# Middle up projection as seven half-size products per pair, from its seventh pair on

## The chip, the cores and the metric

One Trainium2 chip, one of its cores. The metric is device time of one execution in microseconds (us), lower is better. The kernel before has a median of 2146.22 us over 3 runs (2146.05 to 2146.76).

## The reference, cut to what matters

The reference is two transformer blocks in float32 on 512 tokens of width 1024. It has three feed-forward layers; the change is in the second of them, the first of block two:

```python
D_FF_2 = 2816

def swiglu(x, w_gate, w_up, w_down):
    return (jax.nn.silu(x @ w_gate) * (x @ w_up)) @ w_down

def second_block(x, ffn1_norm, ffn1_w_gate, ffn1_w_up, ffn1_w_down, mix_norm, w_in, ...):
    h = rms_norm(x, ffn1_norm[l])
    x = x + 0.5 * swiglu(h, ffn1_w_gate[l], ffn1_w_up[l], ffn1_w_down[l])   # up1, down1
    h = rms_norm(x, mix_norm[l])
    z = h @ w_in[l] + b_in[l]                                               # wq, wk, wv, ...
    ...
    h = rms_norm(x, ffn2_norm[l])
    x = x + 0.5 * swiglu(h, ffn2_w_gate[l], ffn2_w_up[l], ffn2_w_down[l])   # up2, down2
    return rms_norm(x, final_norm)
```

## The kernel before, in words

**Number format.** Every dense product is three matmuls: weights and activations are each split into a rounded part and a rest ("hi" and "lo", type fp32r), and hi·hi, hi·lo and lo·hi are summed in PSUM (`dense`, L965, with the matmuls at L1034, L1037 and L1038; L1007, L1010 and L1017 for the four chunks that run abreast). TensorE gets the products in program order.

**Weights.** They come as a stream of 512 KB slabs (8 tiles of 128x128). SyncE loads slab after slab into four raw buffers (L803) and waits until the one four slabs ago was split (`wait_raw_free`, L686). ScalarE rounds a slab into `w_hi` (L1759, `feed_to`) and GpSimd subtracts to get `w_lo` (L880). Five slabs of `w_hi`/`w_lo` form a ring. ScalarE's instruction order is written out by hand: `silu_of(c)` (L1944) first feeds slabs up to chunk 2c+3, then waits for its input.

**The up projection of a feed-forward.** 44 output chunks of 128 rows, in 22 pairs (gate, value). A chunk is 8 tiles times 3 matmuls on 512 columns. Chunks 0 to 3 run abreast (k outermost), the others one by one, each with one slab. The input is written before its norm factor is known, so VectorE multiplies each output by that factor (`gate_of` L2674, `value_of` L2679), ScalarE takes the silu (L1952), VectorE the product (L2686), ScalarE rounds it into `a_hi` (L1942) and VectorE makes `a_lo` (`low_a`, L2670). Six PSUM banks are used in turn (L717).

**The seven-product form.** The last feed-forward, `up2`, does its pairs from the fifth on in another way (`paired`, L1045): the 256-token halves of the input and the k-halves of the two weight columns form a 2x2 block product, which is done in seven products of half the size in place of eight (each 4 tiles times 3 matmuls on 256 columns, L1058 to L1060). It needs sums and differences of the weight halves, made for each pair (VectorE `pair_one`, `pair_two`, `pair_four`, L2635 to L2652, and the rests at L2657; GpSimd `pair_pool`, L818, the difference "three" at L836 and four rests at L822; ScalarE seven roundings at L1765), and sums of the input halves, made once: VectorE `input_sums` (L2620, L2630), ScalarE `sum_hi_of` (L1794, L1797), GpSimd four rests `s_lo` (L831), which stand in GpSimd's order ahead of the first pair's "three". It also needs the input with its norm factor in it: `scale_input` (L2609, L2612) writes `u_all`, ScalarE rewrites `u_hi`, VectorE rewrites `u_lo` (`input_lo`, L2614, L2618). Outputs from the sixth pair on are kept whole and split late (`apart`, L1990 and L2718), so the down projection reads hi and lo the other way round there (`turned_from`, L966).

Both helpers have a branch for a layer whose input is rewritten only ahead of its first seven-product pair (`unscaled == paired_from`, L1964, L1979, L2708, L2711, L2713); the kernel before does not take it. In it, ScalarE does for the last pair ahead of the switch, in this order (L1969 to L1986):

```python
if c == paired_from - 1:
    pair_raw(p, 2); pair_three(p); pair_two(p); pair_one(p); pair_four(p)
silu_of(c)
if c == paired_from - 1:
    pair_raw(p, 6); pair_raw(p + 1, 0)
    ...
    f(u_hi[:, i, :], u_all[:, i, :], ACT.Copy)      # for the 8 parts
```

`pair_three` waits for GpSimd's "three"; VectorE's `gate_of` of that pair stands behind its `pair_four_lo` (L2705, L2707). TensorE's first seven-product pair waits for its banks, one of which holds that pair's gate chunk (L1068), and for the first four parts of the rewritten `u_lo` (L1073).

Of the kernel before, what the change touches and what calls it, by code (L numbers as in the profile page):

```python
# [27 lines left out]
DC = D // P  # L28
# [16 lines left out]
FC = FF // P  # L45
# [5 lines left out]
KEPT_FROM = 5  # L51
# [59 lines left out]
NSLABS = -(-TILES // SLAB)  # L111


PAIRED = {"up2": (4, FC)}
PAIRS = [(name, c) for name, (lo, hi) in PAIRED.items() for c in range(lo, hi)]
LAYER_OF = {"up": 0, "up1": 1, "up2": 2}
BLOCKS = 7
# [85 lines left out]
def build(nc, t):  # L203

    ctx = ExitStack()
    with ctx:  # L206
# [13 lines left out]
        u_hi = at("u_hi", 72 * KB, [DC, S], F32R)  # L220
        u_lo = at("u_lo", 88 * KB, [DC, S], F32R)
# [106 lines left out]
        r_sb = arena("r_sb", 86, [S])  # L328
# [557 lines left out]
        def _(pe):  # L886
# [829 lines left out]
            stay_busy(10)  # L1716
            sum_last("post2")
            stay_busy(15)
            dense("up1", u_hi, u_lo, (u_ready, 4 * DC), row="pre2", row_at=(4, 4))
            dense("down1", a_hi, a_lo, (a_ready, FC))  # L1720
            dense("wq", u_hi, u_lo, (u_ready, 5 * DC), row="pre3", row_at=(0, 2), again=6 * DC)
            dense("wk", u_hi, u_lo)
            dense_tokens("wv", 2)
            window()
# [13 lines left out]
                    pe.wait_ge(mh_ready, 8)  # L1738
                dense(f"proj_m{m}", m_hi, m_lo)
            dense("out", mg_hi, mg_lo, (mg_ready, 0))  # L1740
            dense("up2", u_hi, u_lo, (u_ready, 7 * DC), row="pre4", row_at=(0, 2), again=8 * DC, upto=8)
            paired("up2", 8 * DC)
            dense("down2", a_hi, a_lo, (a_ready, 2 * FC), row="pre5", row_at=(DC - 1, FC - 2), turned_from=KEPT_FROM)
            stay_busy(7)
            sum_last("pre5")
# [3 lines left out]
        def _(act):  # L1749
# [102 lines left out]
            def rewrite_hi(k0, name, read, scaled, sums=False):  # L1852

                slabs = (START[name][0] + 4 * DC - 1) // SLAB + 1
                for c in range(DC):
                    feed_to(slabs + 1 + c // 2)
                    act.wait_ge(ux_done, k0 + c + 1)
                    if c < DC - 2:
                        act.wait_ge(u_read, read + c + 1)
                    else:  # L1860
                        act.wait_ge(dense_done, group_of(name, 0 if c == DC - 2 else 3))
                    f(u_hi[:, c, :], scaled[c % len(scaled)], ACT.Copy).then_inc(u_part, 1)
                for i in range(4 if sums else 0):
                    sum_hi_of(name, i)
# [490 lines left out]
            factor("post2", misc[2], misc[2])  # L2355

            late_act(2, 16, "ffn1", "up1")
            ffn_swiglu(1, "up1")
            late_act(3, 24, "mix2", "wq", "down1")
            rewrite_hi(DC + 4, "wq", DC - 2, [slot[4][:, :], slot[5][:, :]])  # L2360
            act.dma_start(wvb[:, :], t["wvb"]).then_inc(c_loaded, 16)
            act.dma_start(band[:, :], t["band"]).then_inc(c_loaded, 16)
            for c in range(8):
# [167 lines left out]
                    act.wait_ge(mg_in, m)  # L2531
                    f(mg_hi[:, m - 1, :], ma[:, m - 1, :], ACT.Copy).then_inc(mg_part, 1)
            late_act(4, 32, "ffn2", "up2", "out")
            rewrite_hi(2 * DC + 4, "up2", 2 * (DC - 2), [u_all[:, c, :] for c in range(DC)], sums=True)
            ffn_swiglu(2, "up2", *PAIRED["up2"], 2)
            norm_act(5, 40, "down2")

# [2 lines left out]
        def _(dve):  # L2540
# [7 lines left out]
            def rewrite(gain, k0, factor, scaled):  # L2548

                for c in range(DC + 1):  # L2550
                    if c < DC:
                        if c >= 2:
                            dve.wait_ge(u_ready, k0 + c - 1)
                        STT(scaled[c % 2][:, :], h[:, c, :], V(gain, c), factor[:, :], ALU.mult, ALU.mult)\
                            .then_inc(ux_done, 1)
                    if c >= 1:
                        dve.wait_ge(u_part, k0 + c)
                        TT(u_lo[:, c - 1, :], scaled[(c - 1) % 2][:, :], u_hi[:, c - 1, :].bitcast(F32),
                           ALU.subtract).then_inc(u_ready, 1)
# [54 lines left out]
            def input_lo(k0):  # L2614

                for c in range(DC):
                    dve.wait_ge(u_part, k0 + c + 1)
                    TT(u_lo[:, c, :], u_all[:, c, :], u_hi[:, c, :].bitcast(F32), ALU.subtract).then_inc(u_ready, 1)  # L2618
# [161 lines left out]
            def add_half(name, scale, norm, late=None):  # L2780

                for c in range(DC):
                    if c >= 2:
                        add_squares(norm, c - 1)
                    dve.wait_ge(dense_done, group_of(name, c))
                    STT(h[:, c, :], out_bank(name, c)[:, :], scale, h[:, c, :], ALU.mult, ALU.add).then_inc(h_ready, 1)  # L2786
                    if late:
                        late_lo(c, *late)
                if norm not in LAST_APART:
                    add_squares(norm, DC - 1)  # L2790
# [414 lines left out]
            TT(sq[(DC - 1) % 3][:, :], mo_a[:, DC - 1, :], mo_a[:, DC - 1, :], ALU.mult).then_inc(ms_sq, 1)  # L3205
            post_apply(2, "ple_post", mo_a, "pre2", "ffn1", 4 * DC)
            inverse("pre2")
            ffn_gate(1, "up1")
            add_half("down1", 0.5, "pre3", ("mix2", 5 * DC))
            inverse("pre3")  # L3210
            rewrite("mix2", 6 * DC, r_sb, slot[4:6])
            for c in range(8):
                dve.wait_ge(dense_done, group_of("wq", c))
                if c < 4:
# [177 lines left out]
            for m in range(DC):  # L3392
# [6 lines left out]
                TT(ma[:, m, :], ma[:, m, :], slot[2 + m % 2][:, :], ALU.add).then_inc(mg_in, 1)  # L3399
                dve.wait_ge(mg_part, m + 1)  # L3400
                TT(mg_lo[:, m, :], ma[:, m, :], mg_hi[:, m, :].bitcast(F32), ALU.subtract).then_inc(mg_ready, 1)
            add_half("out", 0.5, "pre4", ("ffn2", 7 * DC))
            inverse("pre4")
            scale_input("ffn2", misc[3])
            input_lo(8 * DC)
            input_sums("up2", 3 * DC + 4)
            ffn_gate(2, "up2", *PAIRED["up2"], 2)
            add_half("down2", 0.5, "pre5")

# [159 lines left out]
```

## Time and profile before

| | us |
|---|---|
| median of 3 runs | 2146.22 |
| span of the profiled execution | 2144.6 |
| time outside that span, by the median | 1.6 |
| `up1`: first matmul of chunk 0 to first of `down1` (two chains of 22 pairs) | 914.7 to about 1155 |
| `up2`: seven-product pairs | 1828.1 to 2011.8 |

Of the profiled execution itself only the span is shown; the 1.6 us are the distance of the median to it. In a timeline row the first number is the start, the second the duration (of a merged row, from the first start to the last end), then engine, line, operation, and in brackets the engine's idle time before it with what ended it.

### The profile page before, as it was taken

The page shows a single profiled execution, that of the slowest core. Times are in us where ns is not written, and L with a number is a line of the kernel's source. Part 1 is how long each engine was busy: PE and PEld are TensorE (multiplying, and loading weights), DVE is VectorE, ACT ScalarE, POOL GpSimd, SP SyncE. Part 2 cuts the span into 40 slices and gives each one's busy share as a digit, 9 for nine tenths or more (in the row PEclk, how much of TensorE's full clock was granted, in tenths as well). Part 3 has the DMA queues.
Part 4 walks back from the last instruction along what each step waited for, and adds up shares of the span by engine and source line. Part 5 has one row for each costly group of instructions (what it writes and reads, how often), then busy time and mean ns, then how long its engine had stood idle before and what let it go on. Part 6 is the DMA issues. An engine that isn't in the chain of part 4 may idle for free. (4 is left out here: it accounts for less than half of the span.)

```text
span 2144.6 us, 29184 instructions
## 1 busy us (share of the span) xinstructions
PE 2122.6 (99%) x11584; PEld 1775.6 (83%) x11584; DVE 1002.8 (47%) x1821; ACT 942.4 (44%) x1630; POOL 946.4 (44%) x441
## 2 busy tenths in 40 slices
PE   9999999999999999999999999999999999999998
PEld 8788877787888888888888888778888888999986
DVE  7684555446655500563332124653744126776611
ACT  7835545545544422442223232662447235545521
POOL 4423322345544443654444344034524445766631
PEclk9999999999999999999999999999999999999999
DMA  4313321232333332222333323023332332333321
GB/s 179 98 50 112 110 69 50 98 113 85 104 94 97 115 102 88 89 89 94 95 97 99 98 89 112 21 79 100 108 89 62 107 93 85 99 103 113 117 92 49
DMA packets 56439, 200.68 MB, mean 94 GB/s; under 512 B 6640, under 2 KB 7536, under 8 KB 55920
## 3 DMA queue, kind: packets, MB, share of 16 engines
q1 hardware_dynamic: 52416, 188.77, 27.8%
q10 hardware_dynamic: 3888, 10.05, 1.4%
q8 instruction: 92, 1.51, 0.3%
q14 instruction: 43, 0.35, 0.1%
HBM read 194.60 MB, written 2.10 MB: 92 GB/s over the span
## 5 line engine op out<-in xcount | busy, mean ns | idle before, releaser
L880 POOL TENSOR_TENSOR w_lo<-raw,w_hi 128x1024 fp32r<-128x1024 f32 x313 | 768.1, 2466 | 1016.0 <-ACT w_hi L1759 988.1
L1759 ACT ACTIVATE w_hi<-raw 128x1024 fp32r<-128x1024 f32 x316 | 326.7, 1051 | 138.2 <-PE dense L1038 84.7
L1034 PE MATMUL dense<-u_hi,w_hi 128*128 128x512 f32 x608 | 237.3, 390 | 0.0
L1038 PE MATMUL dense<-u_hi,w_lo 128*128 128x512 f32 x608 | 236.6, 389 | 0.0
L1037 PE MATMUL dense<-u_lo,w_hi 128*128 128x512 f32 x584 | 227.2, 389 | 0.0
L1034 PE MATMUL dense<-a_hi,w_hi 128*128 128x512 f32 x400 | 156.0, 390 | 0.0
L1037 PE MATMUL dense<-a_lo,w_hi 128*128 128x512 f32 x400 | 155.6, 389 | 0.0
L1038 PE MATMUL dense<-a_hi,w_lo 128*128 128x512 f32 x400 | 155.6, 389 | 0.0
L1034 PE MATMUL misc<-u_hi,w_hi 128*128 128x512 f32 x368 | 143.5, 390 | 0.0
L1038 PE MATMUL misc<-u_hi,w_lo 128*128 128x512 f32 x368 | 143.2, 389 | 0.0
L1037 PE MATMUL misc<-u_lo,w_hi 128*128 128x512 f32 x360 | 140.1, 389 | 0.0
L1034 PEld LDWEIGHTS dense<-u_hi,w_hi 128*128 128x128 f32 x608 | 114.1, 188 | 24.3 <-ACT mo_a L2349 0.4
L1038 PEld LDWEIGHTS dense<-u_hi,w_lo 128*128 128x128 f32 x608 | 114.1, 188 | 23.9
L1037 PEld LDWEIGHTS dense<-u_lo,w_hi 128*128 128x128 f32 x584 | 109.6, 188 | 22.8
L2786 DVE SCALAR_TENSOR_TENSOR h<-dense,h 128x512 f32<-128x512 f32 x24 | 16.6, 691 | 212.9 <-PE dense L1038 212.9
L822 POOL TENSOR_TENSOR w_lo<-raw,w_hi 128x512 fp32r<-128x512 f32 x54 | 70.2, 1314 | 56.2 <-ACT w_hi L1765 56.2
L1037 PEld LDWEIGHTS dense<-a_lo,w_hi 128*128 128x128 f32 x400 | 75.1, 188 | 15.9 <-issue 0.2
L1038 PEld LDWEIGHTS dense<-a_hi,w_lo 128*128 128x128 f32 x400 | 75.1, 188 | 15.7
L1034 PEld LDWEIGHTS dense<-a_hi,w_hi 128*128 128x128 f32 x400 | 75.1, 188 | 15.6 <-issue 0.2
L958 PE MATMUL misc<-u_hi,w_hi 128*128 128x512 f32 x192 | 81.6, 425 | 0.0
L1034 PEld LDWEIGHTS misc<-u_hi,w_hi 128*128 128x128 f32 x368 | 69.1, 188 | 14.7 <-issue 0.4
L1038 PEld LDWEIGHTS misc<-u_hi,w_lo 128*128 128x128 f32 x368 | 69.1, 188 | 14.5
(571 smaller groups left out, 5004.7 us busy)
## 6 DMA issues: line engine op xcount, KB each, us to landing
raw<-in_weights SPq DMA_DIRECT2D x352, 512.0 KB, 3.5
h<-in_x SPq DMA_DIRECT2D x4, 512.0 KB, 6.7
alibi<-in_alibi ACTq DMA_DIRECT2D x1, 2048.0 KB, 8.4
h<-in_x ACTq DMA_DIRECT2D x2, 1024.0 KB, 7.1
out<-result SPq DMA_DIRECT2D x8, 256.0 KB, 2.2
p_raw<-in_p ACTq DMA_DIRECT2D x2, 512.0 KB, 3.2
hn<-mqk ACTq DMA_DIRECT2D x4, 256.0 KB, 4.0
mqk<-mqk ACTq DMA_DIRECT2D x4, 256.0 KB, 3.8
```

The costliest lines, as they stand in the source:

```text
L822: nc.gpsimd.tensor_tensor(piece(w_lo, p, i), src, piece(w_hi, p, i).bitcast(F32), ALU.subtract).then_inc(st_pool, 1)
L880: nc.gpsimd.tensor_tensor(w_lo[:, ring(s), :, :], raw[:, s % RAWS, :, :], w_hi[:, ring(s), :, :].bitcast(F32), ALU.subtract).then_inc(w_sp ...
L958: mm(out, hi, src_hi[:, i, :], start=(i == 0), stop=False)
L1034: first = mm(out, hi, x_hi, start=(i == 0), stop=False)
L1037: mm(out, hi, x_lo, start=False, stop=False)
L1038: last = mm(out, lo, x_hi, start=False, stop=(i == k - 1))
L1759: f(w_hi[:, ring(s), :, :], raw[:, s % RAWS, :, :], ACT.Copy).then_inc(w_part, 1)
L2786: STT(h[:, c, :], out_bank(name, c)[:, :], scale, h[:, c, :], ALU.mult, ALU.add).then_inc(h_ready, 1)
```

## The change

`up1` gets the seven-product form from its pair 6 (the seventh) on, so 16 of its 22 pairs; its first 12 chunks stay as they are, on the unscaled input. The branch with `unscaled == paired_from` comes into use, chunk 11 reports its reads of `u_hi` (`last_reads`), `down1` reads kept chunks turned, and the counts of the later semaphores are moved by one rewrite of the input. Since `PAIRED` lists `up1` now, `down1`'s banks become 2, 3, 0, 1 (L726), where they were 3, 0, 1, 2.

```diff
-PAIRED = {"up2": (4, FC)}
+PAIRED = {"up1": (6, FC), "up2": (4, FC)}
...
-            dense("up1", u_hi, u_lo, (u_ready, 4 * DC), row="pre2", row_at=(4, 4))
-            dense("down1", a_hi, a_lo, (a_ready, FC))
-            dense("wq", u_hi, u_lo, (u_ready, 5 * DC), row="pre3", row_at=(0, 2), again=6 * DC)
+            dense("up1", u_hi, u_lo, (u_ready, 4 * DC), row="pre2", row_at=(4, 4), upto=2 * PAIRED["up1"][0],
+                  last_reads=2 * PAIRED["up1"][0] - 1)
+            paired("up1", 5 * DC)
+            dense("down1", a_hi, a_lo, (a_ready, FC), turned_from=KEPT_FROM)
+            dense("wq", u_hi, u_lo, (u_ready, 6 * DC), row="pre3", row_at=(0, 2), again=7 * DC)
...
-            ffn_swiglu(1, "up1")
+            ffn_swiglu(1, "up1", *PAIRED["up1"], PAIRED["up1"][0])
...
-            ffn_gate(1, "up1")
-            add_half("down1", 0.5, "pre3", ("mix2", 5 * DC))
+            ffn_gate(1, "up1", *PAIRED["up1"], PAIRED["up1"][0])
+            add_half("down1", 0.5, "pre3", ("mix2", 6 * DC))
```

The lines left out move semaphore counts of later stages (`rewrite_hi`, `rewrite`, `input_lo`, `input_sums`, the `dense` and `paired` calls of `up2`) and nothing else.

## Rows read from the trace of the kernel before

**Rows 1.** The page: busy time, share of the span and instructions of each engine.
```profile
PE 2122.6 (99%) x11584; PEld 1775.6 (83%) x11584; DVE 1002.8 (47%) x1821; ACT 942.4 (44%) x1630; POOL 946.4 (44%) x441
```

**Rows 2.** Busy time by stretch: `up1` with whole products, `up2` with seven (columns PE, PEld, DVE, ACT, POOL, clock, DMA).
```profile
942.00:982.00 40.00, 40.00 (x179) 33.09 (x178) 14.85 (x21) 15.21 (x21) 19.40 (x9) 1.00 0.36 111
1850.00:2000.00 150.00, 150.00 (x1252) 150.00 (x1251) 104.36 (x194) 73.58 (x149) 100.05 (x74) 1.00 0.33 103
```

**Rows 3.** VectorE's timeline: the same step of consecutive pairs, `up1` and `up2`.
```profile
965.41 0.70 DVE L2677 TENSOR_TENSOR dense<-dense,r_sb 128x512 f32<-128x512 f32 x1 [2.70 <-PE dense L1038]
976.29 0.70 DVE L2677 TENSOR_TENSOR misc<-misc,r_sb 128x512 f32<-128x512 f32 x1 [2.70 <-PE misc L1038]
...
1860.19 0.42 DVE L2727 TENSOR_TENSOR slot<-misc,slot 128x256 f32<-128x256 f32 x1 [0.81 <-PE misc L1060]
1870.27 0.42 DVE L2727 TENSOR_TENSOR slot<-dense,slot 128x256 f32<-128x256 f32 x1 [0.81 <-PE dense L1060]
```

**Rows 4.** VectorE's timeline in `up1`: after the second pair's product, and the fourth pair's gate.
```profile
947.78 0.68 DVE L2672 TENSOR_TENSOR a_lo<-slot,a_hi 128x512 fp32r<-128x512 f32 x1
950.43 0.69 DVE L2672 TENSOR_TENSOR a_lo<-slot,a_hi 128x512 fp32r<-128x512 f32 x1
```

**Rows 5.** VectorE's timeline ahead of `up2`'s pairs: scaled input, rewritten rests, sums, first difference.
```profile
1790.65 5.36 DVE L2612 SCALAR_TENSOR_TENSOR u_all<-h,vec,misc 128x512 f32<-128x512 f32 x8 [2.69 <-ACT misc L1933]
1795.93 3.40 DVE L2618 TENSOR_TENSOR u_lo<-u_all,u_hi 128x512 fp32r<-128x512 f32 x4
...
1808.35 1.21 DVE L2630 TENSOR_TENSOR s_all<-u_all 128x1024 f32<-128x1024 f32 x1
...
1813.00 0.69 DVE L2677 TENSOR_TENSOR dense<-dense,r_sb 128x512 f32<-128x512 f32 x1
...
1820.55 2.90 DVE L2641 TENSOR_TENSOR misc<-raw 128x512 f32<-128x512 f32 x1
...
1824.68 1.72 DVE L2672 TENSOR_TENSOR a_lo<-slot,a_hi 128x512 fp32r<-128x512 f32 x1
```

**Rows 6.** ScalarE's timeline ahead of `up2`'s pairs: sums rounded, weight parts, silu.
```profile
1810.85 3.33 ACT L1797 ACTIVATE s_hi<-s_all 128x1024 fp32r<-128x1024 f32 x3 [0.20 <-DVE s_all L2630]
...
1824.62 0.63 ACT L1765 ACTIVATE w_hi<-slot 128x512 fp32r<-128x512 f32 x1 [2.27 <-POOL slot L836]
...
1827.83 0.60 ACT L1765 ACTIVATE w_hi<-misc 128x512 fp32r<-128x512 f32 x1 [1.60 <-DVE misc L2652]
```

**Rows 7.** ScalarE's timeline in `up1`: slabs of chunks 10 and 11 rounded.
```profile
956.27 2.00 ACT L1759 ACTIVATE w_hi<-raw 128x1024 fp32r<-128x1024 f32 x2
```

**Rows 8.** GpSimd's timeline: adds beside VectorE, chunk 9's slab, then `up2`'s sums and "three".
```profile
917.31 10.24 POOL L860 TENSOR_TENSOR h<-h,slot 128x512 f32<-128x512 f32 x6 [11.81 <-DVE slot L2591]
...
951.25 2.39 POOL L880 TENSOR_TENSOR w_lo<-raw,w_hi 128x1024 fp32r<-128x1024 f32 x1 [4.59 <-ACT w_hi L1759]
...
1812.08 10.80 POOL L831 TENSOR_TENSOR s_lo<-s_all,s_hi 128x1024 fp32r<-128x1024 f32 x4 [4.81 <-ACT s_hi L1797]
1822.85 1.74 POOL L836 TENSOR_TENSOR slot<-raw 128x512 f32<-128x512 f32 x1
```

**Rows 9.** TensorE's timeline in `up1`: the first matmuls of chunks 9 and 12.
```profile
965.21 0.39 PE L1034 MATMUL dense<-u_hi,w_hi 128*128 128x512 f32 x1
...
981.53 0.39 PE L1034 MATMUL dense<-u_hi,w_hi 128*128 128x512 f32 x1
```

**Rows 10.** The end: busy time by stretch after the last matmul, columns as in rows 2.
```profile
2135.20:2140.30 5.10, 0.00 (x0) 0.00 (x0) 3.78 (x6) 1.24 (x2) 0.00 (x0) 1.00 0.43 161
2140.30:2144.60 4.30, 0.00 (x0) 0.00 (x0) 1.58 (x3) 0.00 (x0) 0.00 (x0) 0.50 0.80 297
```

**Rows 11.** TensorE's timeline in `up2`: the longest of four idle times among its pairs.
```profile
1848.40 0.35 PE L1058 MATMUL dense<-s_hi,w_hi 128*128 128x256 f32 x1 [0.37 <-DVE slot L2767]
```

**Rows 12.** Timeline of all engines where `down1` ends and `wq` begins.
```profile
1275.49 0.69 DVE L2786 SCALAR_TENSOR_TENSOR h<-dense,h 128x512 f32<-128x512 f32 x1 [12.12 <-PE dense L1038]
...
1275.74 0.39 PE L1007 MATMUL dense<-u_hi,w_hi 128*128 128x512 f32 x1
```

More of the change, by code:

```diff
@@ L1740, in _ @@
             dense("out", mg_hi, mg_lo, (mg_ready, 0))
-            dense("up2", u_hi, u_lo, (u_ready, 7 * DC), row="pre4", row_at=(0, 2), again=8 * DC, upto=8)
-            paired("up2", 8 * DC)
+            dense("up2", u_hi, u_lo, (u_ready, 8 * DC), row="pre4", row_at=(0, 2), again=9 * DC, upto=8)
+            paired("up2", 9 * DC)
             dense("down2", a_hi, a_lo, (a_ready, 2 * FC), row="pre5", row_at=(DC - 1, FC - 2), turned_from=KEPT_FROM)
@@ L2357, in _ @@
             late_act(2, 16, "ffn1", "up1")
-            ffn_swiglu(1, "up1")
+            ffn_swiglu(1, "up1", *PAIRED["up1"], PAIRED["up1"][0])
             late_act(3, 24, "mix2", "wq", "down1")
-            rewrite_hi(DC + 4, "wq", DC - 2, [slot[4][:, :], slot[5][:, :]])
+            rewrite_hi(2 * DC + 4, "wq", 2 * DC - 3, [slot[4][:, :], slot[5][:, :]])
             act.dma_start(wvb[:, :], t["wvb"]).then_inc(c_loaded, 16)
@@ L2533, in _ @@
             late_act(4, 32, "ffn2", "up2", "out")
-            rewrite_hi(2 * DC + 4, "up2", 2 * (DC - 2), [u_all[:, c, :] for c in range(DC)], sums=True)
+            rewrite_hi(3 * DC + 4, "up2", 3 * DC - 5, [u_all[:, c, :] for c in range(DC)], sums=True)
             ffn_swiglu(2, "up2", *PAIRED["up2"], 2)
@@ L3207, in _ @@
             inverse("pre2")
-            ffn_gate(1, "up1")
-            add_half("down1", 0.5, "pre3", ("mix2", 5 * DC))
+            ffn_gate(1, "up1", *PAIRED["up1"], PAIRED["up1"][0])
+            add_half("down1", 0.5, "pre3", ("mix2", 6 * DC))
             inverse("pre3")
-            rewrite("mix2", 6 * DC, r_sb, slot[4:6])
+            rewrite("mix2", 7 * DC, r_sb, slot[4:6])
             for c in range(8):
@@ L3401, in _ @@
                 TT(mg_lo[:, m, :], ma[:, m, :], mg_hi[:, m, :].bitcast(F32), ALU.subtract).then_inc(mg_ready, 1)
-            add_half("out", 0.5, "pre4", ("ffn2", 7 * DC))
+            add_half("out", 0.5, "pre4", ("ffn2", 8 * DC))
             inverse("pre4")
             scale_input("ffn2", misc[3])
-            input_lo(8 * DC)
-            input_sums("up2", 3 * DC + 4)
+            input_lo(9 * DC)
+            input_sums("up2", 4 * DC + 4)
             ffn_gate(2, "up2", *PAIRED["up2"], 2)
```

## The prediction

> **What bounds the kernel now.** I read the page first: TensorE is busy 99% of the span [rows 1]. So the time changes by what TensorE's stream becomes shorter, and by the holes it gets; other engines' work costs nothing until TensorE waits for it. Next I compared the two forms of an up projection by stretch. With whole products the weight loads fill 33.1 of 40 us; with seven products per pair they fill 150.0 of 150 us and the matmuls start every 0.120 us (150 / 1252) [rows 2]: that form is bound by loading weights, not by columns. Then I took the length of a pair in each form from the same step of consecutive pairs, and last followed the four engines by their timelines around the point where `up2` changes form, because `up1` will have such a point.
>
> **The gain.** A pair now takes 976.29 − 965.41 = 10.88 us [rows 3], with 48 matmuls of 512 columns. A pair in seven products takes 1870.27 − 1860.19 = 10.08 us [rows 3], 84 matmuls of 256 columns. That is 0.80 us, and 16 pairs give **−12.8 us**. In that form VectorE is busy 104, GpSimd 100 and ScalarE 74 of 150 us [rows 2], with TensorE never short, so the steady part should behave alike in `up1`.
>
> A rule speaks for more. The Trainium skill (TensorE: Matmul & The Clock Gate, Back-to-back issue gap) gives 262 cycles at 2.4 GHz for 256 columns and 518 for 512; an estimate by that page is 10.36 and 9.17 us per pair and a gain of 19.1 us. The rows of this very shape say 10.88 and 10.08, and they decide.
>
> **The switch, step by step.** All times are on the clock of before; up to 947.78 nothing differs [rows 4]. The question is when TensorE may begin the first seven-product pair; it is ready for it at 981.53, where chunk 12 begins now [rows 9].
>
> - VectorE: behind the second pair's product come the 8 multiplies of `scale_input`, 5.36 us [rows 5], to 953.1. The postponed `low_a`, then the third pair's three operations take what they take now, 950.43 − 947.78 = 2.65 us [rows 4], to 955.8. `input_sums` takes 1813.00 − 1808.35 = 4.65 us [rows 5], to 960.4.
> - ScalarE rounds the last sum by 1.2 us later (1814.18 against 1813.00) [rows 5, 6], at 961.6. Behind that wait stands its feeding of weights: chunk 9's slab (1.0 us, half of the merged pair [rows 7]) is rounded at 962.6, where GpSimd splits it at 951.25 now [rows 8]. Split there it takes 2.39 us and ends at about 965.1; TensorE wants it at 965.21 [rows 9]. So the slack of 11 us is used up: cost 0 to 0.7 us (a restart), I take **+0.2**.
> - ScalarE goes on with a silu and two roundings (about 0.53 apart, so 1.6 us) and the slabs of chunks 10 and 11 (2.00 us), to 966.2. In the kernel before it rounded these from 956.27 [rows 7], 8 us earlier. GpSimd splits 9, 10 and 11 one behind the other, to about 970.
> - GpSimd's four `s_lo` stand behind chunk 11. In `up2` they take 10.80 us [rows 8] with VectorE reading SBUF beside them; at the bare 2.39 us they would take 9.56. VectorE has half as much to do here, so I take 10.2, to 980.2. "Three" takes 1.74 there [rows 8], about 1.3 alone, to **981.5**. This is where TensorE is ready already.
> - From "three" on, `up2` needs from 1824.59 to 1828.43, 3.84 us, until ScalarE's rounding of the fourth difference is done [rows 6, 8]; 0.55 of it is VectorE held in a `low_a` [rows 5], so 3.3, to 984.8. Only then come the rest of the fourth difference (0.6), the gate's scaling (0.7) and the silu (0.6): 986.8. In `up2` the gate has no scaling and TensorE does not wait for this silu. ScalarE rounds two more weight parts (1.1) and begins to rewrite `u_hi` (0.6): 988.5. VectorE follows with four `u_lo` at 0.85 each (3.40 for four [rows 5]): **992.0**.
>
> TensorE therefore stands from 981.5 to 992.0: **+10.5 us**. The lower end takes 9.56 for the sums and 0.61 for each `u_lo`: 8.9. The upper takes 10.80 and 1.74, and for each `u_lo` the 1.71 of GpSimd's adds that alternate with VectorE's (10.24 / 6 [rows 8]): 14.9. I take the middle values since VectorE's own work is thin there.
>
> **What follows the hole.** At the kernel's end the granted clock is still 1.00 for 5.1 us without a matmul and 0.50 (1.2 GHz) from then on [rows 10]. A hole of 10.5 us is longer, so the first products will run at half speed. How soon the clock returns, no row here shows: bounds are 0 and a whole pair (10.1 us). I take as long as the fall took, half of it lost, **+2.5 us**, being nearest to the one change of clock that is shown.
>
> In `up2` the first two pairs have three short waits, the longest 0.37 us idle [rows 11], and the last pair has one. VectorE starts late here too (eight `u_lo` and a product ahead of `pair_one_lo`), but slow matmuls cover that: **+0.5** (0 to 1.5) for the first pairs, and **+0.5** (0.3 to 0.6) for the last.
>
> `down1` ends in bank 1 now, not 2. `wq`'s second chunk wants bank 1 at 1275.74, and the last add that frees it runs from 1275.49 to 1276.18 [rows 12]: **+0.4** (0.3 to 0.6). Kept chunks and turned operands change no count of matmuls in `down1`; `up2`'s own switch to `down2` shows them covered. The slab stream carries the same bytes; a pair's second slab can be loaded once chunk 9 is split and is waited for by `pair_one` only, well ahead of "three".
>
> **Sum.** −12.8 + 0.2 + 10.5 + 2.5 + 0.5 + 0.5 + 0.4 = **+1.8 us**. On the profiled execution 2144.6 becomes 2146.4; the median stands 1.6 us above its span, so **2148.0**. This case's own range is 2144 to 2152.
>
> **Rivals.**
> - *The switch is as smooth as `up2`'s (faster).* If "three" came by about 970, silu and rewrite would run under chunk 11. Left are four waits as in `up2`, none above 0.37 us [rows 11] (1.5), and the bank (0.4): −12.8 + 1.9 = −10.9, 2135.3. For it: the same helpers switch `up2` with hardly a wait. Against: there "three" ended 3.5 us ahead of TensorE's first product and the input had been rewritten much earlier; here the sums hold up ScalarE's feeding, and GpSimd's 9.6 us of sums stand behind that feeding. It holds only if I have the order of the slabs wrong by two.
> - *VectorE's rewrite is shut out by GpSimd (slower).* Place: the four `u_lo` from 988.5 on, while GpSimd works off the second pair's "three" and rests. A VectorE operation with both inputs in SBUF took 2.90 us beside `s_lo` [rows 5], a `low_a` 1.72 [rows 5]. At 1.71 each, TensorE starts 3.4 us later: +5.2, 2151.4. It decides from about 1.5 us each. The Trainium skill (SBUF — State Buffer, Who interferes with whom) says such an operation fully waits for GpSimd's to end, not that both get slower; by that page each rest would lose up to a GpSimd operation, and those two rows agree. Against: GpSimd has only four such operations ready at that time.
> - *The skill's matmul pitch holds.* The gain would be 6.3 us larger: 2141.7. The rows speak against it.
>
> **Chances.** Forecast 0.60, smooth switch 0.20, shut-out rewrite 0.18, matmul pitch 0.02. A measurement of this kernel can tell about 0.2% (4.3 us) from no change: under 2141.9 is faster, over 2150.5 slower. The forecast passes 2150.5 with a clock that returns late, 0.07 of its 0.60. So slower 0.18 + 0.07 = 0.25, faster 0.22, same 0.53. The range goes from the smooth switch, 2135, to 2152; outside lie half of the smooth switch and the ends of the two late cases, under 0.2.
>
> **What would show it.** Right: the timeline has one hole of some 10 us on TensorE ahead of the first 256-column matmul of `up1`, ended by a `u_lo` of VectorE; ScalarE idle until GpSimd's "three" just before; the granted clock at 0.5 as matmuls resume; then 10.08 us per pair. Wrong: no hole over 4 us, or pairs longer than 10.1 us throughout, or waits in `down1`.

## The result and the profile after

The changed kernel took **2149.39 us** (median of 18 runs, 2148.82 to 2150.63), the kernel before, run beside it, 2146.36 us (18 runs, 2145.84 to 2148.20). The ratio is 1.0014, with a 95% interval of 1.0008 to 1.0021: 3.0 us longer, which is surely more than nothing and less than the 0.2% that the prediction set as its bound for "slower". The forecast was 2148.0 us. The profiled execution took 2148.82 us with a span of 2147.0 us, 2.4 us over the span of before. One of the 11 runs of experiment 12 below took 4257 us, about twice the others, for a reason that is not on record; its ratio leaves that run out, its median of 2142.65 us counts it (2142.29 without).

TensorE does more instructions in less busy time; the page's first line of after, against [rows 1]:

```profile
PE 2112.9 (98%) x12160; PEld 1794.6 (84%) x12160; DVE 1102.7 (51%) x2001; ACT 990.0 (46%) x1754; POOL 993.1 (46%) x493
```

Busy time fell by 9.7 us and the span grew by 2.4, so TensorE stands idle some 12 us longer. Where, is shown by TensorE's timeline of after. Below, pair 0 is the first seven-product pair (the seventh pair of `up1`), and a product is one of the seven of a pair, 12 matmuls. The rows are the first matmul of pair 0, the first of its fourth product, one in the last pair and the first for `wq`'s second chunk (line numbers are those of each run's own kernel; the column in brackets is the idle time before the instruction and what ended it):

```profile
992.77 0.55 PE L1058 MATMUL dense<-u_hi,w_hi 128*128 128x256 f32 x1 [11.37 <-DVE u_lo L2620]
...
999.57 0.36 PE L1058 MATMUL dense<-s_hi,w_hi 128*128 128x256 f32 x1 [0.43 <-issue]
...
1154.20 0.36 PE L1058 MATMUL dense<-u_hi,w_hi 128*128 128x256 f32 x1 [0.33 <-DVE slot L2757]
...
1277.93 0.50 PE L1007 MATMUL dense<-u_hi,w_hi 128*128 128x512 f32 x1 [0.33 <-DVE h L2788]
```

The last dense product starts at 981.01; at its pitch of 0.23 us the next would be due at 981.24. The hole is 11.5 us. The stretches of after (columns as in rows 2) show the clock and the steady part:

```profile
982.00:990.00 8.00, 0.00 (x0) 0.00 (x0) 4.84 (x6) 5.57 (x12) 5.82 (x6) 0.79 0.29 89
990.00:995.00 5.00, 2.23 (x10) 2.26 (x11) 5.00 (x6) 2.49 (x5) 3.27 (x2) 0.50 0.16 67
995.00:1000.00 5.00, 4.57 (x32) 4.40 (x30) 4.96 (x8) 1.27 (x3) 1.30 (x1) 0.81 0.00 0
...
1010.00:1150.00 140.00, 140.00 (x1169) 140.00 (x1169) 97.16 (x181) 68.92 (x139) 90.80 (x68) 1.00 0.32 106
```

From 1010 to 1150 us TensorE never waits and a matmul starts every 0.120 us (140 / 1169), as in `up2` [rows 2]: the saving per pair is there in full. The granted clock fell inside the hole to 0.50, which is the lower level, 1.2 GHz; the first 18 matmuls of pair 0 ran at a pitch of about 0.213 us.

Who makes the hole is read from the other engines' timelines, in order of time:

```profile
960.74 1.04 ACT L1761 ACTIVATE w_hi<-raw 128x1024 fp32r<-128x1024 f32 x1
961.86 7.56 POOL L880 TENSOR_TENSOR w_lo<-raw,w_hi 128x1024 fp32r<-128x1024 f32 x3 [15.47 <-ACT w_hi L1761]
969.38 10.36 POOL L831 TENSOR_TENSOR s_lo<-s_all,s_hi 128x1024 fp32r<-128x1024 f32 x4
979.70 1.29 POOL L836 TENSOR_TENSOR slot<-raw 128x512 f32<-128x512 f32 x1
981.02 0.63 ACT L1767 ACTIVATE w_hi<-slot 128x512 fp32r<-128x512 f32 x1 [8.05 <-POOL slot L836]
...
983.70 0.60 ACT L1767 ACTIVATE w_hi<-misc 128x512 fp32r<-128x512 f32 x1 [1.07 <-DVE misc L2654]
984.94 0.69 DVE L2679 TENSOR_TENSOR misc<-misc,r_sb 128x512 f32<-128x512 f32 x1
985.66 0.60 ACT L1954 ACTIVATE slot<-misc 128x512 f32<-128x512 f32 x1 [1.36 <-DVE misc L2679]
986.15 1.14 ACT L1767 ACTIVATE w_hi<-raw 128x512 fp32r<-128x512 f32 x2
987.19 4.25 ACT L1988 ACTIVATE u_hi<-u_all 128x512 fp32r<-128x512 f32 x8
987.85 8.27 DVE L2620 TENSOR_TENSOR u_lo<-u_all,u_hi 128x512 fp32r<-128x512 f32 x8 [2.22 <-ACT u_hi L1988]
```

GpSimd works without a pause from 961.86 to 980.99 us: three slabs, four low parts of sums, the third piece ("three"). ScalarE idles 8.05 us for that piece. Behind it stands the tail: three more roundings, the gate and Silu of the sixth pair (the expectations call it the sixth chunk), two raw roundings (weight halves that are rounded as they are), then the rewriting of the input. TensorE wants the first four `u_lo`. One by one, beside GpSimd's operations, they are (VectorE's timeline, then GpSimd's):

```profile
987.85 0.83 DVE L2620 TENSOR_TENSOR u_lo<-u_all,u_hi 128x512 fp32r<-128x512 f32 x1 [2.22 <-ACT u_hi L1988]
988.60 1.75 DVE L2620 TENSOR_TENSOR u_lo<-u_all,u_hi 128x512 fp32r<-128x512 f32 x1
990.27 1.75 DVE L2620 TENSOR_TENSOR u_lo<-u_all,u_hi 128x512 fp32r<-128x512 f32 x1
991.95 0.68 DVE L2620 TENSOR_TENSOR u_lo<-u_all,u_hi 128x512 fp32r<-128x512 f32 x1
...
988.08 1.72 POOL L836 TENSOR_TENSOR slot<-raw 128x512 f32<-128x512 f32 x1
989.75 1.71 POOL L822 TENSOR_TENSOR w_lo<-raw,w_hi 128x512 fp32r<-128x512 f32 x1
```

Two of the four lie beside a whole GpSimd operation and take 1.75 us; the first meets only the end of one and takes 0.83, the last meets none and takes 0.68.

### The profile page after: what moved, and what is told of

Read it like the earlier page. It is cut to its first block and busy times, and to the rows that moved or that the text cites. A ratio compares the mean times of both kernels' runs of the same rounds, so it can differ in the third digit from the quotient of the medians.

```text
span 2147.0 us, 30961 instructions
## 1 busy us (share of the span) xinstructions
PE 2112.9 (98%) x12160; PEld 1794.6 (84%) x12160; DVE 1102.7 (51%) x2001; ACT 990.0 (46%) x1754; POOL 993.1 (46%) x493
## 5 line engine op out<-in xcount | busy, mean ns | idle before, releaser
L880 POOL TENSOR_TENSOR w_lo<-raw,w_hi 128x1024 fp32r<-128x1024 f32 x281 | 695.9, 2487 | 914.0 <-ACT w_hi L1761 886.0
L1034 PE MATMUL dense<-u_hi,w_hi 128*128 128x512 f32 x432 | 168.8, 391 | 0.0
L1038 PE MATMUL dense<-u_hi,w_lo 128*128 128x512 f32 x432 | 168.1, 389 | 0.0
L1037 PE MATMUL dense<-u_lo,w_hi 128*128 128x512 f32 x408 | 158.7, 389 | 0.0
L1058 PE MATMUL dense<-s_hi,w_hi 128*128 128x256 f32 x408 | 116.1, 285 | 0.8 <-issue 0.4
L1059 PE MATMUL dense<-s_lo,w_hi 128*128 128x256 f32 x408 | 115.7, 284 | 0.0
L1060 PE MATMUL dense<-s_hi,w_lo 128*128 128x256 f32 x408 | 115.7, 284 | 0.0
L1034 PE MATMUL misc<-u_hi,w_hi 128*128 128x512 f32 x288 | 112.4, 390 | 0.0
L1038 PE MATMUL dense<-a_lo,w_lo 128*128 128x512 f32 x256 | 99.6, 389 | 0.0
L1058 PE MATMUL dense<-u_hi,w_hi 128*128 128x256 f32 x272 | 77.9, 286 | 12.3 <-DVE u_lo L2620 11.4
```

Of the source, the lines that this page charges most:

```text
L880: nc.gpsimd.tensor_tensor(w_lo[:, ring(s), :, :], raw[:, s % RAWS, :, :], w_hi[:, ring(s), :, :].bitcast(F32), ALU.subtract).then_inc(w_sp ...
L1034: first = mm(out, hi, x_hi, start=(i == 0), stop=False)
L1037: mm(out, hi, x_lo, start=False, stop=False)
L1038: last = mm(out, lo, x_hi, start=False, stop=(i == k - 1))
L1058: mm(out, hi[:, k, :], a_h[:, k, :], start=(start and k == 0), stop=False, skip_group_check=True)
L1059: mm(out, hi[:, k, :], a_l[:, k, :], start=False, stop=False, skip_group_check=True)
```

## The experiments

Theory: the steady gain is real, and the switch gives it back because GpSimd's third piece comes late and the rewriting of the input stands behind it in the queues of ScalarE and VectorE. Main rival: the engines' queues are not the cause, but the SBUF read interface that VectorE and GpSimd seem to share, so that work put elsewhere in either queue is late there. All twelve kernels start from the changed one, and their edits act on `up1` only (the code shown leaves out the conditions that keep `up2` in its old order). Times are medians of 11 runs each, with the ratio to the kernel before and its 95% interval; the kernel before stood at 2146.3 to 2146.5 us beside them. The intervals reach about 1.9 us to either side, so a difference of less than that between two experiments is not settled by their medians. A "hole" below is from the start of the last dense product to the start of the first product of pair 0; it is 11.76 us in the changed kernel.

### 1. Slabs rounded ahead of the sums

```
                     if c == 3 and unscaled == paired_from:
+                        feed(name, 2 * c + 2)
                         for i in range(4):
                             sum_hi_of(name, i)
```

> The changed kernel with one line more: ScalarE feeds the slabs of chunks 9 to 11 before it rounds the four input sums, not after. Theory (TensorE's hole of 11.5 us at the switch is GpSimd's order: slabs 9 to 11 late, then four sums, then 'three', and the tail behind 'three'): GpSimd begins the sums at about 963 in place of 969.4, 'three' ends at about 974.6 in place of 981.0, the hole shrinks to about 5 us, the clock stays at full speed or nearly so, and the time falls by 6 to 8 us, to about 2142. Rival 1 (the tail alone sets the hole: VectorE's rewriting of the input is shut out by GpSimd): 'three' comes earlier but the rewriting still ends at about 992, the time stays within 1 us of 2149.4. Rival 2 (TensorE waits for the last unscaled gate and its silu, which need chunk 10): the hole shrinks by about 2 us only, 2147.

Measured: 2146.43 us (ratio to before 1.0001, 0.9992 to 1.0010), 3.0 us under the changed kernel, with a hole of 9.01 us. That is half or less of the 6 to 8 us that were expected, and by its size it is rival 2's (2147). But the gate of the last dense pair, which that rival names, still stands behind the third piece: it starts at 982.54, 3.95 us after that piece ends, as in the changed kernel (984.94 after 980.99). VectorE's and GpSimd's timelines of this run say why:

```profile
955.39 1.22 DVE L2633 TENSOR_TENSOR s_all<-u_all 128x1024 f32<-128x1024 f32 x1
956.22 9.34 POOL L880 TENSOR_TENSOR w_lo<-raw,w_hi 128x1024 fp32r<-128x1024 f32 x3 [9.48 <-ACT w_hi L1761]
956.64 3.32 DVE L2633 TENSOR_TENSOR s_all<-s_all,u_all 128x1024 f32<-128x1024 f32 x1
959.88 3.42 DVE L2633 TENSOR_TENSOR s_all<-u_all 128x1024 f32<-128x1024 f32 x1
963.23 3.42 DVE L2633 TENSOR_TENSOR s_all<-u_all,s_all 128x1024 f32<-128x1024 f32 x1
...
965.53 11.80 POOL L831 TENSOR_TENSOR s_lo<-s_all,s_hi 128x1024 fp32r<-128x1024 f32 x4
977.30 1.29 POOL L836 TENSOR_TENSOR slot<-raw 128x512 f32<-128x512 f32 x1
```

GpSimd began 5.6 us earlier, but its splits now lie beside VectorE's sums. In the changed kernel, where GpSimd idles beside it, the third of these operations reads (VectorE's timeline of after):

```profile
957.39 1.22 DVE L2632 TENSOR_TENSOR s_all<-u_all 128x1024 f32<-128x1024 f32 x1
```

The same subtraction that takes 1.22 us there takes 3.42 beside the splits, longer by 2.2, about one GpSimd operation (2.39 in [rows 8]). Both engines lose, and the third piece gains 2.4 us of the 5.6. The Trainium skill (SBUF — State Buffer, Who interferes with whom) says that a VectorE instruction with two SBUF inputs contends with a GpSimd instruction that reads SBUF, and that the one which comes second waits for the whole of the other; the rows agree.

### 2. TensorE kept busy in the hole

```
+            pe.wait_ge(up_act, plain_no(1, 3))
+            for _ in range(44):
+                mm(bank[0][:, 0:P], ones[:, :], ident[:, :], start=True, stop=True)
             paired("up1", 5 * DC)
```

> The changed kernel with 44 small matmuls (128x128, into a bank that is free) ahead of the first seven-product pair, about 10.3 us of them, so that TensorE works through the hole; their output is used nowhere. Theory (the clock fell to 1.2 GHz in the hole and its return costs 1.8 us: 18 matmuls 0.213 us apart in place of 0.120): the granted clock stays 1.00, the first pair runs at 0.120 us, the hole ends where it did (992.8), and the time falls by 1.5 to 2 us, to about 2147.6. Rival (the slow matmuls only hid waits that the first pair has anyway): the clock stays up, but waits of about as much appear inside the first two pairs, and the time moves by less than 0.7 us.

Measured: 2148.55 us (1.0009, 1.0000 to 1.0018), 0.8 us under the changed kernel. The clock stayed at 1.00 from 980 to 1150 us, so what the slow clock cost net is about 0.8 us by the medians, which their intervals don't settle, and 0.4 by the traces (the table below); TensorE's timeline has waits in its place:

```profile
992.96 0.36 PE L1058 MATMUL dense<-u_hi,w_hi 128*128 128x256 f32 x1 [1.59 <-DVE u_lo L2623]
...
996.47 0.35 PE L1058 MATMUL dense<-u_hi,w_hi 128*128 128x256 f32 x1 [0.41 <-DVE u_lo L2623]
...
999.29 0.36 PE L1058 MATMUL dense<-s_hi,w_hi 128*128 128x256 f32 x1 [1.15 <-issue]
```

The fifth to eighth `u_lo` and VectorE's first sum of pair 0 arrive no or hardly earlier than before (the sum starts at 998.77, in the changed kernel at 999.06); products at half speed were hiding that. The rival of this run was mostly right.

### 3. GpSimd held back while VectorE makes the first four low parts

```
+                if p == 0:
+                    pool.wait_ge(u_ready, 5 * DC + 4)
                 low(6, raw_half(p, 1, 1), 7)
```

> The changed kernel with one wait more: GpSimd holds back its last rest of the first pair, and with it the second pair's operations, until VectorE has rewritten the first four parts of the input's rest. Theory of the shut-out (each of these four takes 1.2 us in place of 0.6 because GpSimd reads SBUF beside it): the four take 2.4 us, not 4.8, TensorE begins at about 990.4 in place of 992.8, the hole is 9.2 us, and the time falls by about 2 us, to 2147.3. Rival (the four are paced by ScalarE's rounding of the other half, 0.53 us apart, and by their own 0.6 us): no change of the hole, the time stays within 0.7 us or grows, as GpSimd is late for the second pair.

Measured: 2149.54 us (1.0015, 1.0007 to 1.0024), no gain. The hole shrank to 9.55 us, so the first four `u_lo` did come 2 us earlier, but the held work ran into the next four. VectorE's timeline:

```profile
988.27 8.16 DVE L2622 TENSOR_TENSOR u_lo<-u_all,u_hi 128x512 fp32r<-128x512 f32 x8 [2.21 <-ACT u_hi L1990]
...
999.89 0.41 DVE L2752 TENSOR_TENSOR slot<-dense,slot 128x256 f32<-128x256 f32 x1
```

All eight took 8.16 us as against 8.27, and the sum that the fourth product waits for came at 999.89 (999.06 in the changed kernel). TensorE's wait inside the pair grew to 2.43 us from start to start. The first pair is bound by VectorE's whole chain, and a gain at its head alone is given back.

### 4. Raw roundings moved behind the rewriting

```
                     if c == paired_from - 1:
-                        pair_raw(p, 6)
-                        pair_raw(p + 1, 0)
                         if unscaled == paired_from:
...
                                 f(u_hi[:, i, :], u_all[:, i, :], ACT.Copy).then_inc(u_part, 1)
+                            pair_raw(p, 6)
+                            pair_raw(p + 1, 0)
```

> The changed kernel with two of ScalarE's weight roundings moved from before to behind the eight roundings of the rewritten input. Theory (every step between the silu and the fourth rewritten part lies on TensorE's path): the rewriting starts 1.1 us earlier, and since GpSimd's next operation needs one of the two roundings, GpSimd stays quiet beside it, so the four parts take 0.6 us each: TensorE begins at about 989.4 in place of 992.8, the time falls by 3 to 3.5 us, to about 2146. Rival (the rewriting is not what TensorE waits for last; it is a weight part that GpSimd makes): the start stays at 992 or later, and the time does not fall, or grows by the later weight parts.

Measured: 2145.68 us (0.9996, 0.9987 to 1.0005), 3.7 us under the changed kernel, a little more than the 3 to 3.5 expected. The two roundings are 1.14 us of ScalarE's, yet the hole fell by 3.2 us, to 8.51. GpSimd's next operations wait for these roundings, so they no longer meet VectorE's low parts:

```profile
987.32 4.91 DVE L2623 TENSOR_TENSOR u_lo<-u_all,u_hi 128x512 fp32r<-128x512 f32 x8 [1.18 <-ACT u_hi L1989]
```

Eight in 4.91 us, 0.61 each, where the changed kernel took 8.27. Unlike experiment 3 this takes the collision out for all eight.

### 5 and 6. The sums' low parts on VectorE, alone and with late raw roundings

```
 # GpSimd
-                    for i in SUM_ORDER:
+                    for i in SUM_ORDER if name == "up2" else ():
 # VectorE
                         input_sums(name, 2 * DC + 4)
+                    if unscaled == paired_from and c == 3:
+                        for i in SUM_ORDER:
+                            dve.wait_ge(st_hi, sum_no(name, i + 1, BLOCKS))
+                            TT(s_lo[i][:, :, :], s_all[:, i, :, :], s_hi[i][:, :, :].bitcast(F32),
+                               ALU.subtract).then_inc(st_slo, 1)
```

> Theory: GpSimd's queue (three slab splits 7.6 us, then four sum low parts 10.4 us, then the third piece) sets the hole. With the four low parts made by VectorE in its fourth step, the work before the third piece shrinks by 10.4 us less what VectorE's four subtracts (4 x 1.22 = 4.9 us) take from GpSimd in the shared interface: the third piece ends 975 to 976 instead of 981.0, the tail starts while TensorE is still busy, and the hole falls from 11.5 to 3 to 5 us; with the clock kept or a shorter return, the time is 2139.5 to 2142.5 us. Rival: the interface is the limit and VectorE, held op by op beside the splits, is late with the subtraction for piece 1 and with the last gates; the hole stays above 6.5 us and the time at 2144 to 2147 us.

Measured: 2147.92 us (1.0008, 0.9999 to 1.0017), 1.5 us under the changed kernel, hole 10.26 us. The theory missed by over 5 us, the rival by a little. Timelines of all engines:

```profile
962.88 9.08 POOL L880 TENSOR_TENSOR w_lo<-raw,w_hi 128x1024 fp32r<-128x1024 f32 x3 [15.52 <-ACT w_hi L1761]
964.00 11.28 DVE L2720 TENSOR_TENSOR s_lo<-s_all,s_hi 128x1024 fp32r<-128x1024 f32 x4
971.92 2.28 POOL L836 TENSOR_TENSOR slot<-raw 128x512 f32<-128x512 f32 x1
...
978.95 0.60 ACT L1954 ACTIVATE slot<-dense 128x512 f32<-128x512 f32 x1 [12.72 <-DVE dense L2679]
...
980.49 0.62 ACT L1767 ACTIVATE w_hi<-slot 128x512 fp32r<-128x512 f32 x1
```

The third piece was ready at 974.20, 6.8 us earlier than in the changed kernel, and ScalarE took it up only 0.5 us earlier. VectorE's four subtractions took 11.28 us beside the splits and the third piece (4.9 at the 1.22 us that this size takes alone), its gate of the fifth pair stood behind them, and ScalarE waited 12.72 us for that gate. One engine's lateness was exchanged for the other's.

> The sums' low parts on VectorE and the two raw roundings behind the input's eight. Theory: with the third piece early, the raw roundings lie before the end of the dense chunks and cost nothing, so moving them too gives 0 to 1 us over the sums alone: 2139 to 2142 us, hole 3 us, which is the rewriting itself (one rounding 0.53 us and four low parts of 0.61 us behind the last dense product). Rival: GpSimd's last low parts still collide with the input's low parts, and the move gives its 3 to 3.7 us again: 2136 to 2139 us.

Measured with experiment 4's edit on top: 2143.84 us (0.9990, 0.9981 to 0.9999), hole 6.98 us: 4.1 us under experiment 5. The rival's mechanism held (the roundings are worth the same again), though its time was 5 us too low, since it started from a hole of 3 us that wasn't there.

### 7 and 8. Edits added up

Experiment 7 joins the edits of 1 and 4, experiment 8 those of 1, 4 and 5.

> Slab split first and raw roundings late, sums on GpSimd as in the changed kernel. Theory: the two act on different parts of the hole (third piece earlier; tail shorter), so their gains add up: 3.0 and 3.7 make 6.7 us, 2142 to 2143.5 us, hole 5.5 to 6.5 us. Rival: both shorten the same wait, and the time stays near that of the raw roundings alone, 2145 to 2146 us.

Measured: 2142.94 us (0.9986, 0.9977 to 0.9994), hole 5.69 us. The gains add: 6.45 us under the changed kernel, against 6.7 expected.

> All three edits. Theory: the hole cannot fall below the rewriting (about 3 us), so this is within 1 us of the sums on VectorE with late raw roundings. Rival: with the slab split first, VectorE's sums and low parts meet GpSimd's splits and the time is 1 to 4 us above it.

Measured: 2144.72 us (0.9991, 0.9982 to 1.0000), hole 7.14 us: 0.9 us over experiment 6, inside the theory's bound, but its reason is false, since the hole is far from 3 us. Against experiment 7, putting the sums on VectorE costs 1.8 us by the medians and 0.9 by the traces. So moving this work from GpSimd to VectorE is worth little either way: it gained 1.5 us alone, 1.8 with late raw roundings, and lost here, all within the intervals.

### 9 and 10. The rewriting ahead of the pair's pieces

```
 # VectorE, sixth pair
+                    if c == paired_from - 1 and unscaled == paired_from:
+                        gate_of(c)
+                        input_lo(5 * DC)
                     if c == paired_from - 1:
                         pair_two_lo(p)
                         pair_four(p)
                         pair_four_lo(p)
...
 # ScalarE, sixth pair
                     silu_of(c)
...
                                 f(u_hi[:, i, :], u_all[:, i, :], ACT.Copy).then_inc(u_part, 1)
+                            pair_three(p)
+                            pair_two(p)
+                            pair_one(p)
+                            pair_four(p)
+                            pair_raw(p, 6)
+                            pair_raw(p + 1, 0)
```

Experiment 10 adds the line of experiment 1.

> Order alone: on VectorE and ScalarE the sixth chunk's gate, its Silu and the input's eight roundings and low parts come ahead of the first pair's pieces 3, 1, 4, 5, 6 instead of behind them; no work is removed. Theory: the rewriting waits for the third piece only because it stands behind it in two queues. Put ahead, it runs beside the last dense chunk (each eighth is free when that chunk has read it), and TensorE's hole is what GpSimd still makes late: its third piece ends near 981 to 983 and the first low part 1.3 us behind it, so the first product starts at 982.5 to 985, a hole of 1 to 4 us, with short waits of under 1 us each in the first pair; the clock stays up or falls briefly, and the time is 2137.5 to 2141 us, ahead of the kernel before. Rival: the input's low parts meet GpSimd's sum parts in the shared interface, both are late, and the pieces behind the rewriting stall the first pair instead; the wait moves into the pair and the time is 2144 to 2148 us.

Measured: 2145.27 us (0.9995, 0.9986 to 1.0004), hole 4.51 us, a little over the theory's 1 to 4. But inside pair 0 there are three more, of 1.55, 2.40 and 0.87 us from start to start: the rival's time and the rival's reason. VectorE's eight low parts lay beside GpSimd's sums and pieces (VectorE's timeline):

```profile
977.77 10.98 DVE L2628 TENSOR_TENSOR u_lo<-u_all,u_hi 128x512 fp32r<-128x512 f32 x8 [1.18 <-ACT u_hi L1990]
```

> The same order, and the slab rounding ahead of the four sums. Theory: the third piece was 2.4 us earlier with that line, GpSimd is now the last cause, so the first product starts up to 2 us earlier than without it and the time is 0 to 2.5 us under it (2136 to 2140 us). Rival: VectorE's sums meet the splits as they did with that line alone, the last gates are late, and the time is 1 to 3 us over it.

Measured: 2143.69 us (0.9986, 0.9977 to 0.9994), 1.6 us under experiment 9, which lies in the theory's 0 to 2.5; its absolute 2136 to 2140 was missed, since experiment 9 had been. TensorE's timeline:

```profile
984.27 0.36 PE L1058 MATMUL dense<-u_hi,w_hi 128*128 128x256 f32 x1 [2.34 <-DVE u_lo L2629]
...
987.19 0.39 PE L1058 MATMUL dense<-s_hi,w_hi 128*128 128x256 f32 x1 [1.25 <-DVE w_lo L2668]
...
991.01 0.36 PE L1058 MATMUL dense<-u_hi,w_hi 128*128 128x256 f32 x1 [2.13 <-POOL w_lo L822]
```

No wait is longer than 2.4 us, and the clock stayed at 1.00 throughout. The third line shows how a named releaser can mislead: GpSimd's operation ended at 990.44, ScalarE's copy of the first product, for which the same product waits too, ran from 990.54 to 990.91 behind five roundings. It, more likely, ended this wait.

### 11. GpSimd's order alone

```
-                    for i in SUM_ORDER:
+                    for i in SUM_ORDER[:2] if name == "up1" else SUM_ORDER:
...
                 low(2, raw_half(p, 0, 1), 2)
+                if p == 0:
+                    for i in SUM_ORDER[2:]:
+                        sum_lo(i)
                 low(3, three, 3)
```

(`sum_lo` is the body of the loop that stood there.)

> GpSimd's order alone: it makes the low parts of two sums, then the third piece and the first two low parts of pair 0, and only then the low parts of the other two sums, which TensorE reads from the fifth product on. Nothing is added or taken away on any engine. Theory: what GpSimd does ahead of the third piece sets the hole. The piece then ends near 975.8 us instead of 981.0, the tail runs some 4 to 5 us earlier, of which the later low parts give back a little to VectorE's subtracts: a hole of 5 to 7 us, and 2142.5 to 2145 us. Rival: the two low parts that now come later meet the input's low parts in the shared interface, which then take 2 us each; the hole stays over 8 us and the time at 2146 to 2149.5 us.

Measured: 2145.99 us (0.9998, 0.9989 to 1.0007), 3.4 us under the changed kernel, hole 8.14 us. The third piece ended at 976.03, as the theory said. Yet the last step was slow: the first `u_lo` began at 982.88, 5 us earlier than in the changed kernel, and the eight took 10.46 us beside the sums that now lay there:

```profile
978.48 4.71 POOL L827 TENSOR_TENSOR s_lo<-s_all,s_hi 128x1024 fp32r<-128x1024 f32 x2
...
982.88 10.46 DVE L2626 TENSOR_TENSOR u_lo<-u_all,u_hi 128x512 fp32r<-128x512 f32 x8 [2.22 <-ACT u_hi L1994]
```

The hole is the rival's; the time fell just between the two.

### 12. All orders together

As in 11, GpSimd makes two sums ahead of the third piece, but it makes the last two only behind VectorE's eight low parts; the sixth pair's gate and Silu come first; pair 0's first copy and first sum come ahead of what can wait.

```
 # GpSimd
                 low(3, three, 3)
+                if p == 0:
+                    pool.wait_ge(u_ready, 6 * DC)
+                    for i in SUM_ORDER[2:]:
+                        sum_lo(i)
 # ScalarE, sixth pair: silu_of, pair_three, pair_two, pair_one, eight u_hi, then
+                            first_copy(p)
+                            pair_four(p)
+                            pair_raw(p, 6)
+                            pair_raw(p + 1, 0)
 # VectorE, sixth pair
+                        gate_of(c)
+                        pair_two_lo(p)
+                        pair_four(p)
+                        input_lo(5 * DC)
+                        first_add(p)
+                        pair_four_lo(p)
+                        pair_one_lo(p)
...
                     value_of(c)
```

> All orders together, with no work moved from one engine to another: GpSimd as in the run before, but its last two low parts of sums wait until VectorE has made the input's eight; sixth chunk's gate and Silu ahead of the first pair's pieces; the first copy and the first sum of pair 0 ahead of ScalarE's raw roundings and of VectorE's last plain product. Theory: what made the switch dear is order and the interface, so with both out of the way the hole is 1 to 2.5 us, the waits in the first pair under 1.5 us together, the clock stays up, and the time is 2136 to 2139.5 us, 7 to 10 us under the kernel before. Rival: the rewriting cannot be put under the dense chunks (its last eighth, its low parts and GpSimd's last sums follow each other), the waits move into the first pair, and the time is 2141.5 to 2145 us, as with the other orders tried.

Measured: 2142.65 us (0.9982, 0.9973 to 0.9991), 6.7 us under the changed kernel, hole 1.62 us. Timelines of VectorE and TensorE:

```profile
980.38 5.13 DVE L2641 TENSOR_TENSOR u_lo<-u_all,u_hi 128x512 fp32r<-128x512 f32 x8
983.25 0.35 PE L1065 MATMUL dense<-u_hi,w_hi 128*128 128x256 f32 x1 [1.23 <-DVE u_lo L2641]
...
989.26 1.67 DVE L2695 TENSOR_TENSOR a_lo<-slot,a_hi 128x512 fp32r<-128x512 f32 x1
990.85 1.75 DVE L2664 TENSOR_TENSOR misc<-raw 128x512 f32<-128x512 f32 x1
992.64 0.70 DVE L2669 TENSOR_TENSOR misc<-raw,misc 128x512 f32<-128x512 f32 x1
993.24 0.42 DVE L2789 TENSOR_TENSOR slot<-dense,slot 128x256 f32<-128x256 f32 x1
993.81 0.55 PE L1065 MATMUL dense<-u_hi,w_hi 128*128 128x256 f32 x1 [3.13 <-DVE slot L2789]
```

The hole is what the theory said, 1 to 2.5 us. The time is the rival's: the waiting moved to the sixth product of pair 0, which wants VectorE's second sum (L2789). That sum stands behind a low part and a difference that ran beside GpSimd's postponed work, at 1.67 and 1.75 us in place of 0.69. Whether that sum could be brought forward as well was not tried.

**What the runs say together.** The medians can't tell the experiments apart below about 2 us, so here is what the switch costs in each trace (one per kernel): the time from the start of the last dense matmul to the start of the first matmul three pairs after pair 0 begins, less the usual pitch (0.23 us, then 252 of 0.120). It holds the hole, the waits in the first pairs and the slow clock.

| | median | hole | switch cost |
|---|---|---|---|
| changed kernel | 2149.39 | 11.76 | 14.1 |
| 1 | 2146.43 | 9.01 | 11.3 |
| 2 | 2148.55 | 11.81 | 13.7 |
| 3 | 2149.54 | 9.55 | 14.6 |
| 4 | 2145.68 | 8.51 | 10.3 |
| 5 | 2147.92 | 10.26 | 12.6 |
| 6 | 2143.84 | 6.98 | 8.8 |
| 7 | 2142.94 | 5.69 | 8.0 |
| 8 | 2144.72 | 7.14 | 8.9 |
| 9 | 2145.27 | 4.51 | 10.1 |
| 10 | 2143.69 | 2.73 | 7.2 |
| 11 | 2145.99 | 8.14 | 11.1 |
| 12 | 2142.65 | 1.62 | 6.7 |

The changed kernel loses 11.5 us in the hole, 0.6 in the pair and 1.8 by the clock. Experiment 12 loses 1.4 + 3.3 + 0.7 and some clock, experiment 10 loses 2.5 + 1.4 + 2.3 + 0.7. Every edit but that of experiment 3 made the switch cheaper, and none brought its cost below 6.7 us, whichever queue came first: a shorter hole came back in part as waits in the pair. It is shown that the order in the queues sets the hole: the same work on the same engines in another order takes it from 11.76 to 1.62 us (experiment 12). It is also shown that each operation is late beside the other engine's; that the interface is the sole cause of that is argued from the durations, since no run took it away. What keeps the last 6.7 us, the interface or the amount of work in the queues, stays open. The whole interval of experiments 6, 7, 10 and 12 lies below the kernel before; 7 needs the fewest lines for its gain.

## Why the prediction was right

It named the sign, the place and the chain behind it, and was 1.4 us too low (2148.0 against 2149.39). Its terms, on the profiled execution:

| term | forecast | measured | from |
|---|---|---|---|
| 16 pairs | −12.8 | −12.8 | the pitch of 0.120 us in the stretch 1010 to 1150 us |
| chunk 9's slab | +0.2 | 0 | no start-to-start step over 0.26 us from 940 to 981 us |
| hole at the switch | +10.5 | +11.5 | 992.77 − 981.24 |
| clock's return | +2.5 | +1.8 | 18 matmuls in 3.98 us, less 18 × 0.120 |
| first pairs | +0.5 | +0.6 | 0.70 from start to start at 999.57, less 0.12 |
| last pair | +0.5 | +0.5 | 0.61 at 1154.20, less 0.12 |
| `wq`'s bank | +0.4 | +0.5 | 0.72 at 1277.93, less 0.23 |
| sum | +1.8 | +2.1 | |

The spans differ by 2.4 us; the remaining 0.3 is not traced. The mechanism was right; that the sum of the terms is within 0.3 us is in part luck, since a hole 1.0 us too short stands against a clock term 0.7 and a slab term 0.2 too large.

- **The gain** of 0.80 us per pair was taken from the shape's own rows, not from a rule, and it held: the rival with the shorter matmul pitch, 2141.7 us, is out.
- **The chain to "three"**: forecast 981.5, measured 980.99. The order of the slabs and the sums on GpSimd was as worked out, at 10.36 us for the sums (10.2 forecast). The rival of a smooth switch, 2135.3 us, fell with it.
- **The tail**: fourth rounding done at 984.30 (984.8 forecast), Silu done at 986.26 (986.8), first `u_hi` done at about 987.8 (988.5). All of it some half a microsecond early.
- **The mis-sized term** is the four `u_lo`: 0.85 us each were taken, 3.4 in all; they took from 987.85 to the first matmul at 992.77, 4.9 us. The step took the mean of a row [rows 5] in which GpSimd was busy for the first 1.05 of 3.40 us only (GpSimd's timeline of before):

```profile
1792.20 4.78 POOL L880 TENSOR_TENSOR w_lo<-raw,w_hi 128x1024 fp32r<-128x1024 f32 x2 [3.13 <-ACT w_hi L1759]
```

  It put the 1.71 of the rival beside that mean as an upper end. The rows of the four show no such middle value: 1.75 us beside a whole GpSimd operation, 0.68 with none, and experiment 4 shows 0.61 from start to start with GpSimd quiet. So the rival of the rewrite shut out by GpSimd was right in kind and in the price of one collision; it counted four collisions where there were two, and came to 3.4 us where 1.5 were lost.
- **The clock**: the hole did take the clock to 0.50, and the loss of 1.8 us lies under the 2.5. But the line counts it beside the pair's waits as if they were separate. Experiment 2 shows that they overlap: without the slow clock the time falls by 0.8 us only (0.4 in the traces), as VectorE's chain is late by nearly as much. The prediction had said of the first pairs that slow matmuls cover their waits; that was right. The 2.5 came from another change of the clock, within bounds of 0 and about 5 us, so its nearness is luck too.
- **Slips that change nothing**: four times 0.85 from 988.5 on ends at 991.9, not 992.0; 16 times 1.19 is 19.0, not 19.1; and the second line of [rows 4] is a rest (`a_lo`), not the fourth pair's gate, while the 2.65 us read from it are right.

## What to carry to other kernels

Where a kernel changes the form of its product half-way, price the change-over apart from the steady part: here 12.8 us of steady gain were given back within 20 us of the timeline. Follow each engine's queue past the point of change, and for each GpSimd operation that lies beside VectorE operations with two SBUF inputs add up to its own time to VectorE's queue (here about 1.1 us for 128x512, 2.2 for 128x1024). When such a switch is late, move waits and roundings behind what TensorE wants first (3.7 us for two lines here) before moving work between VectorE and GpSimd, which gained 1.8 us at most here and lost as much beside the other edits.

## What was not expected

- VectorE and GpSimd took turns, operation by operation. The same 128x1024 subtraction took 1.22 us alone and 3.32 to 3.42 beside splits of 2.39; 128x512 ones went from 0.68 to 1.75 in the changed kernel. So a line that starts GpSimd 5.6 us earlier brought 3.0 us.
- The two roundings moved in experiment 4 are 1.14 us of one engine's time and were worth 3.7, because other engines' work hangs on their position.
- A slow TensorE clock after a hole cost 1.8 us by the count of matmuls and some 0.4 to 0.8 by the time, since it ran while VectorE was the one that was late.
